# Second attention, projecting steps: transposes and values of every third unit joined with the next unit's small products

## The chip, the cores and the metric

The kernel runs on one core of a Trainium2 chip. The metric is device time in microseconds (us) for one execution; the kernel before takes 1373.73 us, the median of 3 runs (1373.12 to 1374.71). The engines of a core work side by side, each through its own instructions in order, and wait for one another by semaphores: TensorE (PE, with its weight loads shown apart as PEld), VectorE (DVE), ScalarE (ACT), GpSimd (POOL), and SyncE (SP), which issues the loads from memory.

## The reference, cut to what matters

Two transformer blocks run one after the other over 512 tokens of width 1024, all in fp32. The change lies in the second block's attention: 8 "fox" heads of width 64 with a forget gate, and 4 "diff" heads, whose weights are the difference of two softmaxes.

```python
h = _modulate(x, ln1_g[l], sh1, sc1)
u = h @ w_in[l]
fq, fk, fv, fg, dq, dk, dv = jnp.split(u, splits, axis=-1)
fq = _rms(heads(fq, FOX_HEADS, HEAD_DIM_2), fox_qk_g[l, 0])      # fk alike
fox_out = _fox_attention(fq, fk, fv, log_f)    # softmax(q k / 8 + decay, causal) @ v
dq = _rms(dq, diff_qk_g[l, 0])                                    # dk alike
diff_out = _diff_attention(dq[:, :, 0], dq[:, :, 1], dk[:, :, 0], dk[:, :, 1], dv, lam, slopes)
            # (softmax(q1 k1 + alibi) - lam * softmax(q2 k2 + alibi)) @ v, causal
mixed = jnp.concatenate([fox_out..., diff_out...], axis=-1)
x = x + g1[:, None, :] * (mixed @ w_out[l])
```

## The kernel before

Large products are made of three: each operand is split into a rounded high part and a low rest (`w_hi`, `w_lo`, `h_hi`, `h_lo`), and hi x hi, hi x lo and lo x hi are added up in PSUM. ACT makes the high parts of a weight chunk (`to_hi`, L680), DVE the low ones (`to_lo`, L1217).

The second attention goes in steps t = 1 to 4 (the loop `for t in range(1, 5)`, which each engine writes out for itself). Step t attends with the heads of set a = t - 1 (two fox heads and one diff head with its two softmaxes) and, while t < 4, projects queries, keys and values of set t. These three are the **projecting steps**. A step has 12 **units** u = 0 to 11; n = 12a + u counts them through. `UNITS2` gives each unit its kind and its block of 128 queries qb = u // 3: u % 3 = 0 is the diff head (kind 2), u % 3 = 1 and 2 are the two fox heads (kinds 0 and 1). A unit of block qb sees (qb + 1) x 128 keys, so units grow in the course of a step.

A unit passes through this pipeline:

- `scores2(n)` on PE (L2121, in the trace `acc<-qk,qk`) writes q k into the banks `acc2` and `acc3`; for the two fox heads both are made at kind 0, none at kind 1;
- `logits2(n)` on DVE (L1797, `s<-acc,...`) adds the bias, finds the maximum and writes the tile `s_2[n % 3]`;
- ACT makes the exponentials in place (L1030, `s<-s,stat`) and their sum;
- `weights2(n)` on DVE divides (and for kind 2 takes the difference), and signals `p2_ready`;
- `turn2(n)` on PE (L2565, `turn<-consts,s`) transposes qb + 1 blocks into the PSUM bank `turn0`. There is one such bank, so `turn2(n)` waits for `pt2_done`, that is until ACT has copied out the transposes of unit n - 1;
- `turn2_copy(n)` on ACT (L980, `pt<-turn`) copies them to `pt_2[n % 3]` and signals `pt2_done`;
- `values2(n)` on PE (`turn<-pt,v` for the diff head, into the bank `turn1`; `ada<-pt,v` for the fox heads, both at kind 1, none at kind 0) multiplies with the values.

On PE the slot of unit u in a projecting step holds `scores2(n)`, `turn2(n - 2)`, `values2(n - 3)`, and then one twelfth of the projection: 12 products of 512 columns, or 24 of 256 from u = 8 on (the values). At the end of the slots u = 2, 4, 6, 8 `head_squares` follows: two products into the bank `norm` over the squares of a projected query or key.

On ACT, unit u holds, in this order: `turn2_copy(n - 2)`; at u = 0 the squares of the last step's diff head (`diff_square`); at u = 8 the `to_hi` of the chunk after the values; the exponentials of unit n; at u = 2 `fox_round(a - 1)` (L984, the high part of the fox heads' output) and at u = 3 `diff_round(a - 1)`; at u = 1 a `to_hi`; at u = 1, 3, 5, 7 the two `square` operations (L696, L697) of what was just projected, which wait for it; at u = 0 and u = 2, 4, 6, 8 `rstd_start`, three operations (L686, L688, L692) that wait for the norm products; at u = 4 a `to_hi`.

On DVE, unit u holds `logits2(n)`, at u = 4, 6, 8 the rest of the squares (L1272, `sq_lo`), `weights2(n - 1)`, at u = 2 the rest of the squares and a `to_lo`, at u = 3, 5, 7, 9 the scaling of a query or key (which frees its projection bank), at u = 3 `fox_rest(a - 1)` (L1779, `m_lo`), at u = 4 `diff_rest(a - 1)`.

Step 4 doesn't project; it makes half of the first output chunk in place of that, in an order of its own.

Of the kernel before, what the change touches and what calls it, by code (L numbers as in the profile page):

```python
# [154 lines left out]
def program(nc, d):  # L155
# [242 lines left out]
    def norm2(t, mi):  # L398

        return N_2 + 4 * t + max(0, t - 1) + mi  # L400
# [68 lines left out]
    with block:  # L469
# [202 lines left out]
        def _(act):  # L672
# [152 lines left out]
            for c in range(1, NKV // 2):  # L825
                u = W_KV // 2 + c
# [186 lines left out]
            for t in range(1, 5):  # L1013
                w0 = W_Q2 + 3 * t
                a = t - 1
                project = t < 4
                for u in range(12):
                    n = 12 * a + u
                    if n >= 2:
                        turn2_copy(n - 2)  # L1020
                    if a >= 1 and u == 0:
                        diff_square(a - 1)
                    if project and u == 8:
                        to_hi(*divmod(w0 + 3, 2))
                    kind, qb = UNITS2[u]
                    width = (qb + 1) * P
                    sets = 2 if kind == 2 else 1
                    act.wait_ge(s2_freed, 16 * a + s_reads(u)[0] + sets)
                    for e in range(sets):
                        ex = nc.scalar.activation(s_2[n % 3][:, e, 0:width], s_2[n % 3][:, e, 0:width], ACT.Exp, scale=-1.0,  # L1030
                                                  bias=stat2[:, 0, n % 2, e:e + 1], accum_out=stat2[:, 1, n % 2, e:e + 1])
                    ex.then_inc(exp2_done, 1)
                    if a >= 1 and u == 2:
                        fox_round(a - 1)
                    if a >= 1 and u == (3 if project else 7):
                        diff_round(a - 1)
                    if t == 4 and u == 5:
                        to_hi(*divmod(W_OUT2 + 1, 2))
                    if project and u == 1:
                        to_hi(*divmod(w0 + 1, 2))  # L1040
                    if project and u in (1, 3, 5, 7):
                        k = norm2(t, u // 2)
                        act.wait_ge(mm_done, 2 * w0 + u // 2 + 1)
                        act.wait_ge(sum_done, k)
                        square(G[u // 2 % 2], sq_hi_2, sq[0])
                    if a >= 1 and u == (0 if project else 1):
                        rstd_start(norm_d(a - 1), NB[:, :], P)
                    if project and u in (2, 4, 6, 8):
                        rstd_start(norm2(t, u // 2 - 1), NB[:, :], 64)
                    if project and u == 4:  # L1050
                        to_hi(*divmod(w0 + 2, 2))
# [152 lines left out]
        def _(dve):  # L1204
# [579 lines left out]
            def diff_last(a):  # L1784
                newton(norm_d(a), P)
                scale_last(norm_d(a), d_out[:, :])
# [89 lines left out]
            for t in range(1, 5):  # L1876
                w0 = W_Q2 + 3 * t
                a = t - 1
                project = t < 4
                for u in range(13):  # L1880
                    n = 12 * a + u
                    if not project and u == 1:
                        rest2(norm_d(a - 1))
                    if u < 12:
                        logits2(n)
                        if project and u in (4, 6, 8):
                            rest2(norm2(t, u // 2 - 1))
                        if n >= 1:
                            weights2(n - 1)
                    if project and a >= 1 and u == 0:  # L1890
                        rest2(norm_d(a - 1))
                    if project and u == 2:
                        rest2(norm2(t, 0))
                    if project and u == 10:
                        dve.wait_ge(s2_freed, 16 * a + s_reads(10)[0])
                        nc.vector.tensor_scalar(consts[:, K_DIST:K_DIST + TOK], consts[:, K_DIST:K_DIST + TOK], SLOPES_D[t] / SLOPES_D[a], None,
                                                ALU.mult).then_inc(dist_scaled, 1)
                        mask_rows(t)
                    if project and u in (2, 12):
                        to_lo(*divmod(w0 + (1 if u == 2 else 3), 2))  # L1900
                    if a >= 1 and u == (1 if project else 2):
                        diff_first(a - 1)
                    if a >= 1 and u == (1 if project else 5):
                        diff_last(a - 1)
                    if a >= 1 and u == (4 if project else 8):
                        diff_rest(a - 1)
                    if project and u in (3, 5, 7, 9):
                        mi = u // 2 - 1
                        kn, tile = norm2(t, mi), qk[t % 2][mi][:, :]
                        scale_first(kn, tile, G[mi % 2][:, :], gains[:, 1 + mi:2 + mi]).then_inc(acc_freed, 1)  # L1910
                        newton(kn, 64)
                        scale_last(kn, tile)
                    if project and u == 6:
                        to_lo(*divmod(w0 + 2, 2))
                    if a >= 1 and u == 3:
                        fox_rest(a - 1)
                    if project and u in (10, 12):
                        v2_copy(t, u // 2 - 5)
# [200 lines left out]
        def _(pe):  # L2119
# [440 lines left out]
            def turn2(n):  # L2560

                pe.wait_ge(p2_ready, n + 1)
                ge(pe, pt2_done, n)
                for b in range(UNITS2[n % 12][1] + 1):
                    turned = nc.tensor.transpose(T0[:, P * b:P * b + P], s_2[n % 3][:, 0, P * b:P * b + P], ident)  # L2565
                turned.then_inc(turn2_done, 1)
# [51 lines left out]
            for t in range(1, 5):  # L2618
                w0 = W_Q2 + 3 * t
                a = t - 1  # L2620
                project = t < 4
                for u in range(12):
                    n = 12 * a + u
                    if u == 0:

                        pe.wait_ge(acc_freed, 2 * w0 - 18)
                        pe.wait_ge(rstd_done, norm2(a, 3) + 1)
                    if project or u < 2:
                        scores2(n)
                    if n >= 2:  # L2630
                        turn2(n - 2)
                    if not project and u in (2, 5, 6, 8, 9):
                        scores2(n + 1)
                    if n >= 3:
                        values2(n - 3)
                    if not project and u == 3:
                        scores2(n + 1)
                    if project:
                        mi, w = u // 2, w0 + u // 4
                        par = w % 2  # L2640
                        if u % 4 == 0:
                            pe.wait_ge(lo_done, w - 1)
                        if u == 10 or (u % 2 == 0 and mi < 5):
                            pe.wait_ge(acc_freed, 2 * w0 + mi - 17)
                        for part in range(2):
                            if mi < 4:
                                kt0 = 4 * (u % 2) + 2 * part
                                last = columns(G[mi % 2][:, :], par, mi % 2, KT, h_hi, h_lo_of, (kt0, kt0 + 1))
                            else:
                                last = rows(G[mi % 2][:, 256 * (u % 2):256 * (u % 2) + 256], par, u - 8, 0, 256, range(4 * part, 4 * part + 4))  # L2650
                        if u % 2 == 1:
                            last.then_inc(mm_done, 1)
                        if u in (2, 4, 6, 8):
                            head_squares(norm2(t, u // 2 - 1), half_r)
                    if t == 4:

                        half = u % 2
                        if u < 2:
                            pe.wait_ge(lo_done, W_OUT2 - 1)
                            pe.wait_ge(acc_freed, 2 * W_OUT2 + half - 17)  # L2660
                        pe.wait_ge(mlo_done, (4, 4, 4, 4, 5, 6)[u // 2])
                        columns(G[half][:, :], W_OUT2 % 2, half, KT, m_hi, m_lo_of, ((0, 4, 1, 5, 2, 6)[u // 2],))
                    if a >= 1 and u == (0 if project else 1):
                        head_squares(norm_d(a - 1), ones_r)
# [224 lines left out]
```

## Time and profile before

| | |
|---|---|
| median of 3 runs | 1373.73 us (1373.12 to 1374.71) |
| the profiled execution, its own time | 1375.31 us |
| its span, first to last instruction | 1373.5 us |
| PE busy | 1364.8 us, 99% |
| PE weight loads busy | 1169.5 us, 85% |
| DVE busy | 1058.7 us, 77% |
| ACT busy | 718.5 us, 52% |
| POOL busy | 51.0 us, 4% |
| projecting steps 1, 2, 3 | about 812.7 to 965.8 us of the span |

How to read it: the span is from the first to the last instruction of the profiled execution; its own time has a little more around it. Busy time is the sum of an engine's instructions; those of PE overlap, since a product is counted until its last result is out, so PE is shown busy even where the distance between two products is longer than it need be. That distance is read from the starts in the timeline. The chain of work that ended last says which engine sets the end. In a timeline a row gives start, duration, engine, line, operation, tiles (out<-in), shapes and count; equal instructions that follow one another are merged, with their number behind x. In square brackets is the time for which the engine stood idle before, and what ended it.

### The profile page before, as it was taken

To read this page: it belongs to the slowest core of one execution; us is meant where nothing else is said; L and a number is where in the kernel's file an instruction comes from. 1 tells how busy PE (TensorE), PEld (TensorE's weight loads), DVE (VectorE), ACT (ScalarE), POOL (GpSimd) and SP (SyncE) were. 2 spreads that over 40 slices of the span, in tenths; PEclk is the share of its full clock that TensorE was granted. 3 is DMA by queue.
4 is the path that set the end of the run, shared out by engine and by line. 5 is a ranking of instruction groups with operands and counts; after the bars stand their busy time and mean duration, and the time that the engine had idled before them with its cause. 6 is when DMAs were issued, how large, how long until landed. Compare 5 with 4: busy or idle time off the path is not lost.

```text
span 1373.5 us, 21419 instructions
## 1 busy us (share of the span) xinstructions
PE 1364.8 (99%) x7923; PEld 1169.5 (85%) x7923; DVE 1058.7 (77%) x1787; ACT 718.5 (52%) x1260; POOL 51.0 (4%) x55
## 2 busy tenths in 40 slices
PE   8999999999999999999999999999999999999999
PEld 6998888888889878888888787787688998998997
DVE  6976777777899788888888877778867965983883
ACT  4744333223357566666663566766646642662561
POOL 0000000000100000000001100000030000000000
PEclk9999999999999999999999999999999999999999
DMA  9994445457743211112212231111131232333232
GB/s 378 382 354 188 177 181 183 183 201 279 293 155 108 93 62 63 62 62 74 78 62 66 88 124 63 64 60 62 48 107 64 91 123 67 119 123 124 69 116 92
DMA packets 35350, 181.51 MB, mean 132 GB/s; under 512 B 4153, under 2 KB 4921, under 8 KB 20930
## 3 DMA queue, kind: packets, MB, share of 16 engines
q1 hardware_dynamic: 34050, 177.95, 35.7%
q10 hardware_dynamic: 1216, 2.44, 0.6%
q8 instruction: 52, 0.85, 0.3%
q14 instruction: 32, 0.26, 0.1%
HBM read 177.74 MB, written 2.11 MB: 131 GB/s over the span
## 4 chain that ended last, share of the span: by engine, by line
PE 97%; DVE 1%; ACT 1%; issue 0%; DMA 0%; DVEq 0%; ACTq 0%
PE acc L2121 72%; PE turn L2708 7%; PE ada L2121 4%; PE turn L2121 3%; PE norm L2121 3%; PE ada L2708 2%; PE acc L2708 2%; PE norm L2708 2%; PE turn L2565 1%; PE turn L2422 1%; DVE y_half L1209 0%; DVE w_lo L1217 0%; DVE wv_lo L1217 0%; ACT sq L697 0%; DVE k_t L1209 0%
## 5 line engine op out<-in xcount | busy, mean ns | idle before, releaser
L2121 PE MATMUL acc<-h_hi,w_hi 128*128 128x512 f32 x696 | 277.8, 399 | 0.0
L2121 PE MATMUL acc<-h_hi,w_lo 128*128 128x512 f32 x696 | 272.0, 391 | 0.0
L2121 PE MATMUL acc<-h_lo,w_hi 128*128 128x512 f32 x696 | 271.3, 390 | 0.0
L1217 DVE TENSOR_TENSOR w_lo<-w_raw,w_hi 128x2048 fp32r<-128x2048 f32 x58 | 136.4, 2352 | 27.7 <-ACT w_hi L680 27.7
L2121 PEld LDWEIGHTS acc<-h_hi,w_lo 128*128 128x128 f32 x696 | 130.6, 188 | 28.4
L2121 PEld LDWEIGHTS acc<-h_hi,w_hi 128*128 128x128 f32 x696 | 131.0, 188 | 27.1 <-issue 1.2
L2121 PEld LDWEIGHTS acc<-h_lo,w_hi 128*128 128x128 f32 x696 | 130.9, 188 | 25.6
L680 ACT ACTIVATE w_hi<-w_raw 128x2048 fp32r<-128x2048 f32 x60 | 114.3, 1906 | 29.4 <-PE acc L2121 28.6
L1209 DVE SCALAR_TENSOR_TENSOR x<-acc,mods,x 128x512 f32<-128x512 f32 x48 | 38.7, 813 | 68.6 <-PE acc L2121 68.6
L2121 PE MATMUL acc<-wv_hi,h_hi 128*128 128x256 f32 x320 | 90.5, 284 | 0.0
L2121 PE MATMUL acc<-wv_lo,h_hi 128*128 128x256 f32 x320 | 89.1, 279 | 0.0
L2121 PE MATMUL acc<-wv_hi,h_lo 128*128 128x256 f32 x320 | 88.3, 279 | 0.0
L686 ACT ACTIVATE y<-norm,eps_tile 128x512 f32<-128x512 f32 x54 | 37.2, 688 | 72.8 <-PE norm L2121 72.8
L2121 PE MATMUL acc<-gu_lo,w_hi 128*128 128x512 f32 x176 | 68.5, 389 | 0.0
L2121 PE MATMUL acc<-gu_hi,w_hi 128*128 128x512 f32 x176 | 68.5, 389 | 0.0
L2121 PE MATMUL acc<-gu_hi,w_lo 128*128 128x512 f32 x176 | 68.5, 389 | 0.0
L2121 PEld LDWEIGHTS acc<-wv_hi,h_hi 128*128 128x128 f32 x320 | 60.1, 188 | 1.2 <-issue 1.0
L2121 PEld LDWEIGHTS acc<-wv_lo,h_hi 128*128 128x128 f32 x320 | 60.9, 190 | 0.2
L2121 PEld LDWEIGHTS acc<-wv_hi,h_lo 128*128 128x128 f32 x320 | 59.6, 188 | 0.0
L1209 DVE SCALAR_TENSOR_TENSOR ada_out<-ada_out,csil 128x1024 f32<-128x1024 f32 x32 | 38.4, 1221 | 17.2 <-DMA ada_out<-in_ada 16.9
L2121 PE MATMUL acc<-y_hi,w_hi 128*128 128x512 f32 x128 | 49.9, 390 | 0.0
L2121 PE MATMUL acc<-y_hi,w_lo 128*128 128x512 f32 x128 | 49.8, 389 | 0.0
(372 smaller groups left out, 3489.8 us busy)
## 6 DMA issues: line engine op xcount, KB each, us to landing
w_raw<-in_weights SPq DMA_DIRECT2D x102, 1024.0 KB, 4.9
ada_v<-in_ada SPq DMA_DIRECT2D x32, 512.0 KB, 6.3
ada_raw<-in_ada SPq DMA_DIRECT2D x32, 512.0 KB, 5.6
ada_out<-in_ada SPq DMA_DIRECT2D x32, 512.0 KB, 6.5
ada_up<-in_ada_first SPq DMA_DIRECT2D x8, 1024.0 KB, 16.3
w_raw<-in_weights SPq DMA_DIRECT2D x4, 768.0 KB, 4.3
x<-in_x SPq DMA_DIRECT2D x2, 1024.0 KB, 6.1
w_first<-in_weights SPq DMA_DIRECT2D x4, 512.0 KB, 13.3
```

Of the source, the lines that this page charges most:

```text
L680: nc.scalar.activation(weights_at(u, par)[0][:, 0:used], w_raw[par][:, 0:used], ACT.Copy).then_inc(hi_done, 1)
L686: nc.scalar.activation(y0[:, :], total, ACT.Ln, scale=1.0 / count, bias=eps_col).then_inc(ln_done, 1)
L1209: return nc.vector.scalar_tensor_tensor(out, in0, scalar, in1, op0, op1, **more)
L1217: nc.vector.tensor_tensor(lo[:, 0:used], w_raw[par][:, 0:used], f32(hi[:, 0:used]), ALU.subtract).then_inc(lo_done, 1)
L2121: return nc.tensor.matmul(out, lhsT, rhs, start=start, stop=stop)
L2422: turned = nc.tensor.transpose((T0, T1)[c % 2][:, P * b:P * b + P], s_b[tile][:, lo:lo + P], ident)
L2565: turned = nc.tensor.transpose(T0[:, P * b:P * b + P], s_2[n % 3][:, 0, P * b:P * b + P], ident)
L2708: last = nc.tensor.matmul(out, w_part[:, n, :], a_part[:, n, :], start=start and n + m == 0, stop=stop and n + m == 5, skip_group_check=no ...
```

## The change

In the projecting steps PE no longer does `turn2` and `values2` in the slots u % 3 = 2. What stood there goes to the head of the next slot: for n = 3, 6, ..., 36, `turn2(n - 3)` and `values2(n - 4)` come ahead of `scores2(n)`, and `turn2(n - 2)` and `values2(n - 3)` follow it as before. So small products stand in 8 of the 12 slots of a step. The unit n = 36 is the first of step 4.

ACT's copy of the transposes that moved goes with them: `turn2_copy(n - 3)` is now the first thing in the units u % 3 = 0, directly ahead of `turn2_copy(n - 2)`, and the units u % 3 = 2 have none. Since the fox heads' last values of a step come one slot later, `fox_round` goes on ACT from u = 2 to u = 3 and `fox_rest` on DVE from u = 3 to u = 4, ahead of `diff_rest`.

```diff
--- before.py
+++ after.py
@@ -1016,7 +1016,9 @@
                 project = t < 4
                 for u in range(12):
                     n = 12 * a + u
-                    if n >= 2:
+                    if 0 < n <= 36 and u % 3 == 0:
+                        turn2_copy(n - 3)
+                    if n >= 2 and not (project and u % 3 == 2):
                         turn2_copy(n - 2)
                     if a >= 1 and u == 0:
                         diff_square(a - 1)
@@ -1030,7 +1032,7 @@
                         ex = nc.scalar.activation(s_2[n % 3][:, e, 0:width], s_2[n % 3][:, e, 0:width], ACT.Exp, scale=-1.0,
                                                   bias=stat2[:, 0, n % 2, e:e + 1], accum_out=stat2[:, 1, n % 2, e:e + 1])
                     ex.then_inc(exp2_done, 1)
-                    if a >= 1 and u == 2:
+                    if a >= 1 and u == (3 if project else 2):
                         fox_round(a - 1)
                     if a >= 1 and u == (3 if project else 7):
                         diff_round(a - 1)
@@ -1902,6 +1904,8 @@
                         diff_first(a - 1)
                     if a >= 1 and u == (1 if project else 5):
                         diff_last(a - 1)
+                    if a >= 1 and project and u == 4:
+                        fox_rest(a - 1)
                     if a >= 1 and u == (4 if project else 8):
                         diff_rest(a - 1)
                     if project and u in (3, 5, 7, 9):
@@ -1912,7 +1916,7 @@
                         scale_last(kn, tile)
                     if project and u == 6:
                         to_lo(*divmod(w0 + 2, 2))
-                    if a >= 1 and u == 3:
+                    if a >= 1 and not project and u == 3:
                         fox_rest(a - 1)
                     if project and u in (10, 12):
                         v2_copy(t, u // 2 - 5)
@@ -2625,13 +2629,18 @@
 
                         pe.wait_ge(acc_freed, 2 * w0 - 18)
                         pe.wait_ge(rstd_done, norm2(a, 3) + 1)
+                    joined = n <= 36 and u % 3 == 0
+                    if joined and n > 0:
+                        turn2(n - 3)
+                        if n > 3:
+                            values2(n - 4)
                     if project or u < 2:
                         scores2(n)
-                    if n >= 2:
+                    if n >= 2 and not (project and u % 3 == 2):
                         turn2(n - 2)
                     if not project and u in (2, 5, 6, 8, 9):
                         scores2(n + 1)
-                    if n >= 3:
+                    if n >= 3 and not (project and u % 3 == 2):
                         values2(n - 3)
                     if not project and u == 3:
                         scores2(n + 1)
```

## Rows read from the trace of the kernel before

**Rows 1.** The page, chain of work that ended last: shares by engine.
```profile
PE 97%; DVE 1%; ACT 1%; issue 0%; DMA 0%; DVEq 0%; ACTq 0%
```

**Rows 2.** Timeline of PE, step 2, slots 0 to 2: start us, us, engine, line, operation.
```profile
865.75 0.40 PE L2121 MATMUL norm<-sq_lo,ones_r 128*128 128x512 f32 x1
...
866.07 0.49 PE L2121 MATMUL acc<-qk,qk 64*128 64x128 f32 x4
...
869.76 0.27 PE L2565 MATMUL turn<-consts,s 128*128 128x128 f32 x1
869.97 1.09 PE L2121 MATMUL ada<-pt,v 128*64 128x128 f32 x16
870.99 0.50 PE L2121 MATMUL acc<-h_hi,w_hi 128*128 128x512 f32 x1
...
871.33 0.40 PE L2121 MATMUL acc<-h_lo,w_hi 128*128 128x512 f32 x1
```

**Rows 3.** Timeline, step 2, slots 2 and 3: all engines.
```profile
871.87 0.69 DVE L1272 TENSOR_TENSOR sq_lo<-sq,sq_hi 128x512 fp32r<-128x512 f32 x1 [1.52 <-ACT sq L697]
...
873.84 0.39 PE L2121 MATMUL norm<-sq_hi,half_r 128*128 128x512 f32 x1
...
874.51 0.69 ACT L686 ACTIVATE y<-norm,eps_tile 128x512 f32<-128x512 f32 x1 [1.63 <-PE norm L2121]
...
875.03 0.33 PE L2565 MATMUL turn<-consts,s 128*128 128x128 f32 x1
...
876.43 0.26 ACT L980 ACTIVATE pt<-turn 128x128 f32<-128x128 f32 x1
```

**Rows 4.** Timeline, after the steps: PE released by DVE.
```profile
993.33 0.70 DVE L1272 TENSOR_TENSOR sq_lo<-sq,sq_hi 128x512 fp32r<-128x512 f32 x1 [0.41 <-ACT sq L697]
...
994.08 0.50 PE L2121 MATMUL norm<-sq_hi,ones_r 128*128 128x512 f32 x1
```

**Rows 5.** Timeline of PE, step 1, slots 2 and 3.
```profile
822.26 0.39 PE L2121 MATMUL norm<-sq_hi,half_r 128*128 128x512 f32 x1
...
823.45 0.33 PE L2565 MATMUL turn<-consts,s 128*128 128x128 f32 x1
```

**Rows 6.** Timeline of ACT and PE, step 2, slots 5 and 6.
```profile
886.19 0.36 ACT L980 ACTIVATE pt<-turn 128x256 f32<-128x256 f32 x1
...
886.45 0.50 ACT L1030 ACTIVATE s<-s,stat 128x256 f32<-128x256 f32 x1
...
886.75 0.44 PE L2565 MATMUL turn<-consts,s 128*128 128x128 f32 x2
...
887.90 0.39 ACT L980 ACTIVATE pt<-turn 128x256 f32<-128x256 f32 x1
```

**Rows 7.** Timeline of ACT and PE, step 2, slots 8 and 9.
```profile
894.70 0.49 PE L2565 MATMUL turn<-consts,s 128*128 128x128 f32 x3
...
895.87 0.50 ACT L980 ACTIVATE pt<-turn 128x384 f32<-128x384 f32 x1
...
896.24 1.93 ACT L680 ACTIVATE w_hi<-w_raw 128x2048 fp32r<-128x2048 f32 x1
...
898.05 0.62 ACT L1030 ACTIVATE s<-s,stat 128x384 f32<-128x384 f32 x1
...
898.55 0.21 ACT L1030 ACTIVATION_READ_ACCUMULATOR s<-s,stat 128x1 f32 x1
...
900.17 0.55 PE L2565 MATMUL turn<-consts,s 128*128 128x128 f32 x3
```

**Rows 8.** Timeline of ACT and PE, step 2 slot 11, step 3 slot 0.
```profile
908.25 0.60 PE L2565 MATMUL turn<-consts,s 128*128 128x128 f32 x4
...
908.88 0.60 ACT L980 ACTIVATE pt<-turn 128x512 f32<-128x512 f32 x1 [1.74 <-PE turn L2565]
...
910.90 0.72 ACT L1030 ACTIVATE s<-s,stat 128x512 f32<-128x512 f32 x1 [1.42 <-DVE stat L1797]
...
912.94 0.66 PE L2565 MATMUL turn<-consts,s 128*128 128x128 f32 x4
```

## The prediction

> **What bounds the kernel now.** First the chain of the page: almost all of it lies on TensorE (PE) [rows 1]. So time is saved only where PE is spared work, and lost wherever PE is made to wait. Then the timeline of PE in the second attention's projecting steps (t = 1, 2, 3; about 51.6 us each: the same norm product, that of slot 2, stands at 822.26 in step 1 and at 873.84 in step 2 [rows 3, 5]). There each of the 12 units of a step is a slot: a group of small products (scores, transposes, values), then 2.74 us of projecting products (from 870.99 to the norm product at 873.84, less the 0.11 explained below), and after some slots two norm products. I write S, T, V for scores, transposes and values, with the unit's number in the step; P for the projecting part; N(u) for the norm products at the end of slot u. The reader is to see that PE runs through from one slot to the next, and what leaving and entering a group costs [rows 2]. Last, the timeline of ScalarE (ACT) in the same stretch, since T is a single PSUM bank: `turn2` waits until ACT has copied the transposes before it (`pt2_done`), and ACT works in its program's order. Where ACT stands when PE wants the bank is the whole question.
>
> **What the change removes.** In each slot with u % 3 = 2, T and V go out and come back at the head of the next slot. The number of S, T, V and P instructions is unchanged. What goes is one passage P to small and one back. From the last norm product to S it is 866.07 - 865.75 = 0.32 us, and within a run of 512-column products one takes (873.84 - 871.33) / 11 = 0.228 [rows 2, 3], so entering S costs 0.09. Leaving costs at least the slower first product, 870.99 to 871.33 = 0.34, that is 0.11 more. V to P and the new V to S, which the trace of before doesn't show, I take as equal, for both leave a form of another shape. Saving: 0.09 + 0.11 = 0.20 us a join. Its bounds are 0 (V to S, with both shapes changed, costs 0.20 more than V to P) and 0.35: 16 V take 1.09, so one follows another by (1.09 - 0.27) / 15 = 0.055 if the last is as long as a T, 0.27; the last begins at 870.79 and P 0.20 later, 0.15 more than a V would, and that too would go if V to S costs nothing. Joins are at n = 3, 6, ..., 36: 12 of them, so 2.4 us, from 0 to 4.2.
>
> A page bears on this. What the rows show is a first S, whose operands have 64 rows, coming 0.32 after a product of 128 rows rather than 0.23. The Trainium skill, TensorEngine Tiling (Array Packing), section Tiling Modes, Key Properties, says that "Changing tiling mode (not just tile) drains the TensorE". Before, slots 2 and 3 change mode four times around T, V, S and T, after it three times. By that rule alone the change is a gain of the size just worked out, and it would be the rival below.
>
> **What the change adds: a wait in the middle of the joined group.** In slot u = 0, 3, 6, 9 PE now does T(n-3), V(n-4), S(n), T(n-2), V(n-3), P. T(n-2) needs ACT's copy of T(n-3). Before, that copy had a whole slot. Now only V(n-4) and S(n) lie between, and in ACT's order the copy has moved from ahead of exp(n-1) to behind everything that ACT does in slot n-1. Queued behind the waiting T on PE are V, P and all later slots, so each wait goes fully into the time. The four places:
>
> u = 3, steps 2 and 3. ACT ends slot 2 with `rstd_start`, three operations that begin with the norm N(2). P(2) now begins where T(0) stood, 869.76 instead of 870.99, and sheds the 0.11: N(2) would come at 873.84 - 1.34 = 872.50. But it needs `sq_lo`, done at 871.87 + 0.69 = 872.56, whose chain on ACT begins before the moved work; with 0.05 from a DVE end to a PE start [rows 4] N(2) is at 872.61. The first operation follows N by 874.51 - 873.84 = 0.67, the copy follows that by 876.43 - 874.51 = 1.92 and takes 0.26 [rows 3]: it ends at 875.46, so T(1) is at 875.51 where it was at 875.03. Lost 0.48, and twice (step 3 repeats step 2): 0.96.
>
> u = 3, step 1. There is no V(-1), and slot 2 held one transpose only, so N moves just by about 0.1, to 822.16. Copy: 822.16 + 0.67 + 1.92 + 0.26 = 825.01, T(1) at 825.06 where it was at 823.45 [rows 5]. Lost 1.61.
>
> u = 6, all three steps. Before, ACT copied T(3) at 886.19, then exp(5), the two squares of the key, and copied T(4) at 887.90 [rows 6]. Now the first copy is gone from its place (0.26 earlier for what follows: 886.45 - 886.19) and stands behind the squares, at 887.90 - 0.26 = 887.64. It takes 0.36, so T(4) is at 888.05 where it was at 886.75. Lost 1.30 each: 3.90. Cover is missing by much, because ACT comes late from rounding a weight chunk at u = 4.
>
> u = 9, all three steps. exp(8) begins 896.24 - 895.87 = 0.37 earlier, at 897.68, and its read of the sum, 0.50 later, takes 0.21: ACT is free at 898.39. N(8) comes with P(8) from 894.70 on at 897.44, its first follower could be at 898.11, so ACT decides: 898.39 + 1.92 + 0.50 for the copy + 0.05 = 900.86, where T(7) was at 900.17 [rows 3, 7]. Lost 0.69 each: 2.07. DVE's `sq_lo` for N(8) and the bank freed for P(8) may be tight as well, as `sq_lo` was at N(2), which can only add; I price that in rival (b).
>
> u = 0 of the next step, three times. Slot 11 has no work of ACT behind exp(11). T(9) would be at 908.25 + 2.74 = 910.99, its copy could start 908.88 - 908.25 = 0.63 later, at 911.62; ACT is at exp(11) from 910.90 for 0.72 and the read, some 0.1 more, so it copies from about 911.75 to 912.35. T(10) is wanted at 912.94 - 0.20 = 912.74 [rows 8]: no wait, the 0.20 is kept. Gain 0.60.
>
> Sum: 0.96 + 1.61 + 3.90 + 2.07 - 0.60 = 7.94 us, say 7.9. The savings at the nine other joins are not added, since T(n-2) is set by ACT there and no longer by PE. The 0.05 per wait is from DVE to PE (994.08 - 993.33 - 0.70 [rows 4]); for ACT to PE the trace shows no wait so clean, and allow 0 to 0.15, that is -0.5 to +0.9 over nine waits.
>
> The rest moves at nothing. `fox_round` and `fox_rest` go one unit later: each is an operation of 512 columns, about 0.69 by the nearest rows [rows 3], on ACT and DVE, and ACT waits for PE once in each of these slots (the 1.63 in [rows 3] is one such wait); m_lo of a fox head is next read a whole step later, and the V that overwrites its bank moved by a slot too. If that cover were gone, 0.7 per step would be late. No DMA is moved; the weight loads wait on DVE's `lo_done` and PE's pace, both of which only get later. Nothing after unit 36 changes in order, so the delay is carried to the end: the later stages have PE as their bound too, and I see no place that gives it back.
>
> **Rivals.** (a) The passages decide, and the copies are hidden: 12 x 0.20 = 2.4 us faster, 1371.3, and up to 4.2, 1369.5, by the other bound. For it: it is so at u = 0, where ACT's slot ends early. Against it: [rows 3, 6, 7], where ACT's own chain is longer than V + S. It decides if the copy of T(n-3) ends before S(n) does, so at u = 6 by 886.5 instead of 888.0. (b) The waits come, but PE also waits where ACT or DVE now have no slack (N(2), N(8), the freed bank at P(8)), and ACT's lateness is carried from one join into the next: twice more per step at up to 0.3, and 0.15 for each released T, about 2.7 us on top: 1384.4. For it: the 0.06 by which `sq_lo` already misses N(2). Against it: each of ACT's stretches begins again with something that PE releases (1.63 of waiting in [rows 3]), so lateness isn't carried. (c) The two sides nearly cancel: the copies are in time at u = 6 (3.90 less, and 0.60 saved) and at u = 3 of step 1 (1.61 less), which leaves 1.8: 1375.6. It would need ACT to be some 1.3 us earlier against PE at both places than its rows have it.
>
> **How the numbers follow.** The profiled execution took 1375.31 us (span 1373.5); plus 7.9 it would be 1383.3, span 1381.4. It stands 1.6 above the median of the runs, 1373.73, and the difference carries over: 1381.7. Chances: my forecast 0.74, (b) 0.15, (a) 0.06, (c) 0.05. The range leaves out (a) and (c) and the tails: below, 1378.7, if u = 6 costs 0.7 instead of 1.3 and u = 3 of the first step 0.9 instead of 1.6 (-2.5) with the smaller gap per wait (-0.5); above, 1385.0, (b) with a little more. A measurement of this kernel can tell about 0.2% (2.75 us) from no change. Slower by more than that: 0.89, from the forecast and (b); within: 0.07, (c) and the part of (a) with 0.20 a join, whose 2.4 us just miss the bound; faster: 0.04, (a) with more than 0.23 a join.
>
> **What would show it.** In the profile after: TensorE's list of waits gets "turn <- ACT pt" with nine entries of about 0.5 to 1.6 us, and the group `turn<-consts,s` the idle time; the T behind S at u = 6 is 1.3 later against its S than before, at u = 9 0.7, at u = 0 it is not. The number of matmuls stays. A step from `turn` to `turn` grows from 51.6 to about 53.9. From V straight to S shows the price of that passage: 0.20 from the last V if my 0.20 a join is right. The forecast is wrong if the copies lie before the squares, if PE has no idle at these places, or if the steps grow by less than 1.

## The result, and the profile after

The changed kernel takes 1381.44 us (median of 6 runs, 1381.32 to 1382.36), the kernel before 1373.14 beside it: 8.3 us slower, a ratio of 1.006 with a 95% interval of 1.0049 to 1.0071. The forecast was 1381.7.

The page of the kernel after, engines and shares of the chain, and then TensorE's list of waits (us in total, times, longest):

```profile
PE 1361.7 (99%) x7923; PEld 1166.6 (85%) x7923; DVE 1058.9 (77%) x1787; ACT 718.5 (52%) x1260; POOL 50.9 (4%) x55
PE 87%; DMA 3%; ACT 3%; DVE 3%; issue 2%; SPq 0%; DVEq 0%; ACTq 0%
```
```profile
PE turn L2569 <- ACT pt L980: 9.2, 9, 1.6
```

The work is the same, PE is still shown 99% busy, but nine waits of T for ACT's copy are new, at the nine places that the sum named. ACT's share of the chain rose from 1% to 3% [rows 1], since the chain goes through ACT wherever T waits. Most of PE's fall from 97% to 87% is something else, which differs from trace to trace: in the run join_u0 below, in which no T waits for a copy in these steps, the chain has these shares:

```profile
PE 90%; DMA 3%; DVE 3%; issue 1%; ACT 1%; SPq 0%; DVEq 0%; ACTq 0%
```

The first and the last S of the second attention tell where the time went. First before, then after; the columns are the durations of one, least/median/most, in ns, and the first and last start in us:

```profile
L2121 PE MATMUL acc<-qk,qk x128: 272/482/693, 812.7 to 985.3; 64*128 64x128 f32 x32, 64*128 64x256 f32 x32, 64*128 64x384 f32 x32, 64*128 64x512 f32 x32
```
```profile
L2125 PE MATMUL acc<-qk,qk x128: 272/482/693, 810.3 to 991.5; 64*128 64x128 f32 x32, 64*128 64x256 f32 x32, 64*128 64x384 f32 x32, 64*128 64x512 f32 x32
```

I call this stretch the stage: 172.6 us before, 181.2 after, 8.6 longer. That is the whole loss of 8.3, to within 0.3. That the stage of before begins 2.4 later is no effect of the change: its profiled execution (1375.31) lost those 2.4 us ahead of the stage, and stands 2.2 above the median of all runs shown beside it, 1373.14. The profiled execution of after, 1381.5, stands at its median. So the step from span to span, 6.2, understates the change, and from here on the stage is compared with the stage.

The timelines of step 2 after, at u = 3, 6, 9 and at u = 0 of step 3, beside [rows 3, 6, 7, 8]:

```profile
873.35 0.39 PE L2125 MATMUL acc<-h_hi,w_lo 128*128 128x512 f32 x1
873.72 0.50 PE L2125 MATMUL norm<-sq_hi,half_r 128*128 128x512 f32 x1
874.06 0.40 PE L2125 MATMUL norm<-sq_lo,half_r 128*128 128x512 f32 x1
874.49 1.09 PE L2125 MATMUL ada<-pt,v 128*64 128x128 f32 x16
874.49 0.69 ACT L686 ACTIVATE y<-norm,eps_tile 128x512 f32<-128x512 f32 x1 [1.17 <-PE norm L2125]
875.51 0.70 PE L2125 MATMUL acc<-qk,qk 64*128 64x256 f32 x4
876.41 0.26 ACT L980 ACTIVATE pt<-turn 128x128 f32<-128x128 f32 x1
876.81 0.30 PE L2569 MATMUL turn<-consts,s 128*128 128x128 f32 x1 [0.59 <-ACT pt L980]
...
887.51 0.92 PE L2125 MATMUL acc<-qk,qk 64*128 64x384 f32 x4
888.95 0.58 ACT L697 ACTIVATE sq<-acc 128x512 f32<-128x512 f32 x1
889.43 0.38 ACT L980 ACTIVATE pt<-turn 128x256 f32<-128x256 f32 x1
889.96 0.41 PE L2569 MATMUL turn<-consts,s 128*128 128x128 f32 x2 [1.53 <-ACT pt L980]
...
901.43 0.68 ACT L686 ACTIVATE y<-norm,eps_tile 128x512 f32<-128x512 f32 x1
903.34 0.47 ACT L980 ACTIVATE pt<-turn 128x384 f32<-128x384 f32 x1
903.96 0.52 PE L2569 MATMUL turn<-consts,s 128*128 128x128 f32 x3 [0.61 <-ACT pt L980]
...
915.46 0.58 ACT L980 ACTIVATE pt<-turn 128x512 f32<-128x512 f32 x1
916.14 0.49 PE L2125 MATMUL acc<-qk,qk 64*128 64x128 f32 x4
916.56 0.66 PE L2569 MATMUL turn<-consts,s 128*128 128x128 f32 x4
```

Read the bracket on T: it can start only when the copy above it is done. At u = 0 there is no bracket; the copy, 915.46 + 0.58, was done before T was wanted. The same T stood at 875.03, 886.75, 900.17 and 912.94 before, so it lies 1.78, 3.21, 3.79 and 3.62 later; from one to the next +1.43, +0.58, -0.17, and +0.65 for the first against the T(10) ahead of it (862.49 after, 861.36 before). Over all three steps, with the forecast in parentheses: u = 3 of step 1 +1.64 (1.61), u = 3 of steps 2 and 3 +0.65 and +0.63 (0.48 each), u = 6 +1.44, 1.43, 1.45 (1.30), u = 9 +0.71, 0.58, 0.64 (0.69), u = 0 -0.25, -0.17, -0.16 (-0.20). Sum 8.6 against 7.94. From one step to the next, the T of u = 3 stands at 876.81 and 930.87, 54.1 apart, where 53.9 were forecast and 51.6 is the value of before.

### The profile page after: what moved, and what is told of

Its sections match the earlier page's. It is cut to its first block, busy times and chain, and to the rows that moved or that the text cites. A ratio compares the mean times of both kernels' runs of the same rounds, so it can differ in the third digit from the quotient of the medians.

```text
span 1379.7 us, 21419 instructions
## 1 busy us (share of the span) xinstructions
PE 1361.7 (99%) x7923; PEld 1166.6 (85%) x7923; DVE 1058.9 (77%) x1787; ACT 718.5 (52%) x1260; POOL 50.9 (4%) x55
## 4 chain that ended last, share of the span: by engine, by line
PE 87%; DMA 3%; ACT 3%; DVE 3%; issue 2%; SPq 0%; DVEq 0%; ACTq 0%
PE acc L2125 64%; PE turn L2717 7%; PE ada L2125 4%; DMA ada_out<-in_ada 3%; PE turn L2125 3%; PE norm L2125 2%; PE ada L2717 2%; PE acc L2717 2%; PE norm L2717 2%; DVE w_lo L1219 1%; PE turn L2569 1%; PE turn L2426 1%; ACT y L686 1%; ACT wv_hi L680 1%; ACT y L688 1%
```

## The experiments

Two theories. **The waits**: TensorE waits straight for ACT's copy, nine times, and each such wait goes in full into the time; without them the change gains what the passages save. **Against it**: my rival (b), that late norms, freed banks and lateness handed on carry a good part; and rival (a), that only passages count. All runs are compared with runs of the kernel before on the same chip. The stage below is from the first to the last S of each run's own trace.

### copies_both: the copies ahead again, the groups still joined

```diff
-                    if 0 < n <= 36 and u % 3 == 0:
+                    if 0 < n <= 36 and u == 0:
                         turn2_copy(n - 3)
-                    if n >= 2 and not (project and u % 3 == 2):
+                    if n >= 2 and not (project and u in (2, 8, 11)):
                         turn2_copy(n - 2)
...
+                    if project and u in (2, 8):
+                        turn2_copy(n - 2)
                     if project and u in (2, 4, 6, 8):
                         rstd_start(norm2(t, u // 2 - 1), NB[:, :], 64)
```

> The changed kernel, its joined groups on TensorE untouched; only ScalarE's order differs: the copy of T(3) stands ahead of exp(5) again, and those of T(0) and T(6) ahead of rstd_start of slots 2 and 8. If the nine waits of TensorE for the copies are the whole loss (8.6 us of the stage), they go, and the passages saved stay, 0.20 each at 12 joins: 1381.4 - 8.6 - 2.4 = 1370.5 us, 2.5 faster than before, and no row of TensorE waiting for pt longer than 0.2. If the loss comes from norms or freed banks that are late (my rival b), at least 2 us of it stay: 1372.5 or more. If passages save nothing, 1373.1.

Measured: 1373.14 us against 1373.20, ratio 1.000 (0.9991 to 1.0009); stage 172.0. The loss is gone with nothing but the order of ACT changed, so the waits were the loss. But the stage is only 0.6 shorter than before and not 2.4. The trace of this run tells why. At the end of slot 2, at u = 6 and at the start of P(8), step 2:

```profile
868.76 0.39 PE L2127 MATMUL acc<-h_hi,w_lo 128*128 128x512 f32 x1
869.13 0.50 PE L2127 MATMUL norm<-sq_hi,half_r 128*128 128x512 f32 x1
869.47 0.39 PE L2127 MATMUL norm<-sq_lo,half_r 128*128 128x512 f32 x1
...
882.22 0.92 PE L2127 MATMUL acc<-qk,qk 64*128 64x384 f32 x4
882.70 0.36 ACT L980 ACTIVATE pt<-turn 128x256 f32<-128x256 f32 x1
883.21 0.41 PE L2571 MATMUL turn<-consts,s 128*128 128x128 f32 x2
...
890.27 0.74 DVE L1213 SCALAR_TENSOR_TENSOR qk<-acc,gains,y 128x512 f32<-128x512 f32 x1
890.88 0.39 PE L2127 MATMUL acc<-h_hi,w_lo 128*128 128x512 f32 x1
891.16 0.36 PE L2127 MATMUL acc<-wv_hi,h_hi 128*128 128x256 f32 x1
```

N(2) comes 0.37 after the last P in place of 0.23, and its second product 0.34 after the first: 0.14 of waiting for the squares, and then 0.11 for a slow first product, as after any break. S to T takes 0.99 in place of 0.84. P(8) begins 0.28 after the last product ahead of it, so 0.05 late, and 0.15 after DVE has freed its bank (890.27 + 0.74), and has 0.08 of a slow first product too. N(8) of step 1 waits for the squares as well, 0.14 in all. And the products of slots 10 and 11 take 5.74 us together, 901.76 to 907.50, where they take 5.55 in the trace of after. That is 2 x 0.25 + 3 x (0.15 + 0.13) + 0.14 + 3 x 0.19 = 2.05 us, of which 0.57 is slower spacing of products, with no wait and no cause found: the saving of 2.4 is eaten almost whole.

### copies_squares and copies_rstd: one kind of place at a time

copies_squares puts only the copy of T(3) back (`u in (0, 3, 9)` and `u in (2, 8, 11)` in the two conditions), copies_rstd only those of T(0) and T(6).

> Of the three places only u = 6 is put right: ScalarE copies T(3) ahead of exp(5), so not behind the two squares. ScalarE is rounding a weight chunk until 886.2 on the axis of the trace before, the copy ends at 886.55, T(4) is wanted at 886.55 and comes at 886.7, 0.05 ahead of its old place, in place of 1.44 behind it: three times 1.5 less, 1377.0 us. The waits at u = 3 and u = 9 stay as long as they are (1.6, 0.65, 0.63 and about 0.65 behind their old places). If waits share a cause and pass from one to the next, those at u = 9 shrink too and it is under 1376.

Measured: 1377.46 us, 4.3 above before (ratio 1.0028, 1.0018 to 1.0038), stage 176.8; T waits 6 times. The gain of 4.4 in the stage is the one expected, and the waits at u = 9 stay.

> Only u = 3 and u = 9 are put right: the copies of T(0) and T(6) stand ahead of the three operations of rstd_start. They were 1.64 + 0.65 + 0.63 and 0.71 + 0.58 + 0.64 = 4.85 behind their old places and come 0.20 ahead of them: 4.85 + 1.2 = 6.0 less, 1375.4 us, the waits at u = 6 unchanged at 1.4 to 1.6. The norm's chain starts up to 0.5 later behind its sums; if that is on the path (the bank of the key, the query of the next step), it is 1376 or more.

Measured: 1377.24 us, 4.0 above before (1.0027, 1.0018 to 1.0036), stage 176.4, 4.8 us less than after where 6.0 were expected. T waits 3 times, S to T at u = 6 is 2.45 as in after. What is missing are again the savings, 0.20 at each join, not the waits. The lists of the two runs, copies_squares first, then copies_rstd:

```profile
PE turn L2569 <- ACT pt L980: 4.6, 6, 1.6
```
```profile
PE turn L2571 <- ACT pt L980: 4.6, 3, 1.5
```

The two add up to the nine waits of after, 4.6 + 4.6 = 9.2: each place stands for itself, and nothing is handed from one to the next. The stage says the same: 4.4 and 4.8 us less than after, and with both orders changed 181.2 - 172.0 = 9.2. That part of rival (b) is out.

### round_later: why ACT is late at u = 6

```diff
+                    if project and u == 6:
+                        to_hi(*divmod(w0 + 2, 2))
...
-                    if project and u == 4:
-                        to_hi(*divmod(w0 + 2, 2))
```

> ScalarE's rounding of the weight chunk moves from u = 4 to u = 6, behind the two copies there; the order of exp(5), squares, copy of T(3) is the changed kernel's. My claim is that ScalarE is late at u = 6 because of this rounding, 1.9 us. Then the squares begin when P(5) is done, the copy ends at about 886.55 on the old axis, T(4) comes at 886.7 in place of 888.2: 4.3 less, 1377.1 us. If the order alone is at fault (copy behind the squares), the wait stays over 1 us and the time within 1 us of 1381.4. If the chunk is now late for P(8), a new wait of TensorE for wv_lo appears at u = 8.

Measured: 1377.62 us (ratio 1.0034, 1.0021 to 1.0047), stage 177.0. The copy still lies behind the squares, yet the waits at u = 6 are gone from the list (6 left, 4.6 us); S to T there is 1.03, where 0.84 is the value of before, so 0.2 is left of each. So the order makes the wait possible and the rounding of the chunk, 1.9 us just before, makes it long. No wait for `wv_lo` appeared.

### extra_op: one more operation ahead of each moved copy

```diff
-            def turn2_copy(n):
...
+            def turn2_copy(n, extra=False):
...
                 act.wait_ge(turn2_done, n + 1)
                 width = (UNITS2[n % 12][1] + 1) * P
+                if extra:
...
+                    nc.scalar.activation(spare[:, :], T0[:, :], ACT.Copy).then_inc(spare_done, 1)
...
-                        turn2_copy(n - 3)
+                        turn2_copy(n - 3, True)
```

> The changed kernel with one more operation of ScalarE, a copy of 512 columns to an unused tile, about 0.48 from its start to the next, ahead of each moved copy (at all 12 joins). If TensorE waits straight for the copy at u = 3, 6, 9, each of these nine waits grows by the whole 0.48, 4.3 us; at u = 0, where the copy had 0.2 to spare by my sum, by 0.25 to 0.3, another 0.8: 1386.5 us in all, 5.1 slower than the changed kernel. If the waits were only partly the copy's, it grows by less than 3 us.

Measured: 1390.98 us (ratio 1.0123, 1.0106 to 1.014), stage 189.0: 9.5 slower than the changed kernel by the medians and 7.8 by the stage, where 5.1 were expected. TensorE's list, and then four of its waits, those of 2.0 or longer, in the timeline:

```profile
PE turn L2577 <- ACT pt L988: 13.6, 9, 2.1
```
```profile
825.94 0.30 PE L2577 MATMUL turn<-consts,s 128*128 128x128 f32 x1 [2.10 <-ACT pt L988]
841.23 0.41 PE L2577 MATMUL turn<-consts,s 128*128 128x128 f32 x2 [2.02 <-ACT pt L988]
896.87 0.41 PE L2577 MATMUL turn<-consts,s 128*128 128x128 f32 x2 [2.02 <-ACT pt L988]
952.53 0.41 PE L2577 MATMUL turn<-consts,s 128*128 128x128 f32 x2 [2.02 <-ACT pt L988]
```

The waits grew by 13.6 - 9.2 = 4.4 us, as expected for a straight wait, and at u = 0 S to T went from 0.42 to 0.53: 0.11 each, 0.3 in all, so the copy there had more to spare than the 0.2 of my sum. The other 3.1 us of the stage are something that no theory had. The windows before, in and after the first wait, behind the second and third of these four, and behind the last, and two products in the third window. A row has the window and its length, the busy us of PE, PEld, DVE, ACT and POOL, the granted clock, the DMA share and GB/s:

```profile
818.00:822.90 4.90, 4.90 (x23) 4.01 (x22) 2.55 (x7) 3.10 (x5) 0.00 (x0) 1.00 0.00 0
823.00:825.90 2.90, 0.84 (x6) 0.30 (x4) 2.86 (x9) 2.60 (x5) 0.00 (x0) 1.00 0.31 45
827.00:830.40 3.40, 3.40 (x9) 2.65 (x9) 0.04 (x1) 0.53 (x3) 0.00 (x0) 0.50 0.32 133
841.40:845.00 3.60, 3.60 (x20) 2.97 (x18) 2.31 (x2) 1.57 (x5) 0.00 (x0) 1.00 0.23 32
897.00:900.50 3.50, 3.50 (x19) 3.00 (x19) 2.35 (x2) 1.58 (x5) 0.00 (x0) 1.00 0.16 21
953.20:956.50 3.30, 3.30 (x10) 2.59 (x9) 1.81 (x1) 1.35 (x5) 0.00 (x0) 0.51 0.24 40
```
```profile
827.52 0.63 PE L2133 MATMUL acc<-h_lo,w_hi 128*128 128x512 f32 x1
827.95 0.63 PE L2133 MATMUL acc<-h_hi,w_lo 128*128 128x512 f32 x1
```

After the first wait, 2.10 us long, and after the last, 2.02, TensorE's granted clock was 0.50 (1.2 GHz), and the products came 0.43 apart in place of 0.23; each time it cost 1.6 us. The two other waits of 2.02, with the same work around them, left the clock at 1.00. In the trace of after, with waits up to 1.61, the clock is 1.00 all along. The four runs of this kernel differ in it: their mean granted clocks are 0.998 (the profiled one), 0.996, 0.997 and 0.999, where every run of every other kernel here has 1.0. So the number of such stretches changes from run to run, and which of these waits brings one is open. That may also be why the medians give 9.5 and the stage of the one trace 7.8, but no run here shows it.

### join_u0: joins only where no wait came

The kernel before with the join at n = 12, 24 and 36 alone, on PE and ACT.

> The kernel before with joins only at u = 0 (n = 12, 24, 36), where no wait for the copy came. Passage theory: 0.20 a join, the stage 0.6 us shorter by its trace, within noise by its time: 1372.6. In copies_both the 48 products of the values that now follow one another in slots 10 and 11 took 5.74 us in place of 5.57. If that comes from running without a break, it shows here too and eats nearly all: the stage no more than 0.1 shorter. If not, spacing in slots 10 and 11 stays 0.114 and the whole 0.6 is there.

Measured: 1372.57 us against 1373.55 (ratio 0.9992, 0.9983 to 1.0001, not told apart from no change), stage 171.9, 0.7 shorter. Taken from the first S to the S of unit 36, which stops ahead of step 4, it is 0.72: 0.24 for each join. V, S and T of this run at the join of step 2:

```profile
860.07 0.88 PE L2123 MATMUL ada<-pt,v 128*64 128x128 f32 x12
860.87 0.49 PE L2123 MATMUL acc<-qk,qk 64*128 64x128 f32 x4
861.29 0.66 PE L2567 MATMUL turn<-consts,s 128*128 128x128 f32 x4
```

The passages do save what was said. And the products in slots 10 and 11 kept their spacing of 0.114, so running without a break is not what slowed them in copies_both.

### fox_late: the part priced at nothing

`fox_round` and `fox_rest` one unit later in the kernel before, nothing else.

> The kernel before with fox_round and fox_rest one unit later and nothing else, the part that I priced at nothing. Cover theory: the stage from its first scores to those of step 4 stays at 151.4 us within 0.1, the time within 0.1% of before. Without cover it would be 0.7 in steps 2 and 3, 1.4 us slower.

Measured: 1373.25 us against 1373.55 (1.0001, 0.9991 to 1.001), stage 172.6, that of before. It costs nothing.

### rounds_moved: the two chunks behind the squares

```diff
-                    if project and u == 1:
-                        to_hi(*divmod(w0 + 1, 2))
                     if project and u in (1, 3, 5, 7):
...
                         square(G[u // 2 % 2], sq_hi_2, sq[0])
+                    if project and u == 1:
+                        to_hi(*divmod(w0 + 1, 2))
+                    if project and u == 5:
+                        to_hi(*divmod(w0 + 2, 2))
...
-                    if project and u == 4:
-                        to_hi(*divmod(w0 + 2, 2))
```

> copies_both, with the two weight chunks of slots 1 and 4 rounded behind the squares of units 1 and 5 in place of ahead of them. In copies_both TensorE lost 0.14 + 0.11 at N(2) of steps 2 and 3 (squares late, then a slow first product) and 0.14 at T(4) of each step, 0.9 us, both through ScalarE rounding a chunk just before. If so, these go: the stage 151.4 - 0.57 - 0.9 = 149.9 us, 1.5 shorter than before, the time about 1371.7, 0.1% faster than before and at the edge of what can be told. If the losses only move to the exponentials of units 2 and 6, the stage stays at 150.8 or more.

Measured: 1371.92 us against 1373.55, ratio 0.9987 (0.9978 to 0.9995), 1.6 us or 0.13% faster than before, and the stage 171.1, 1.5 shorter, as expected. N(2), and S and T at u = 6, of step 2 in this run:

```profile
871.58 0.39 PE L2127 MATMUL acc<-h_hi,w_lo 128*128 128x512 f32 x1
871.81 0.39 PE L2127 MATMUL norm<-sq_hi,half_r 128*128 128x512 f32 x1
...
884.79 0.92 PE L2127 MATMUL acc<-qk,qk 64*128 64x384 f32 x4
885.64 0.44 PE L2571 MATMUL turn<-consts,s 128*128 128x128 f32 x2
```

N(2) follows the last P by 0.23 and T follows S by 0.85, as before the change: neither waits any more. This is the version that beats both kernels, by little. The spacing of the products changed too, but both ways, and nearly cancels: slots 10 and 11 of step 1 have the shorter one again, and slot 8 has the longer one in all steps.

## Why the prediction was right, point by point

**The nine waits.** Right in place, cause and number. Undoing ACT's order alone (copies_both) took the whole loss back, each kind of place answered by itself, and lengthening ACT by one operation lengthened all nine waits by it, 0.49 each.

**Their sizes.** 8.6 in the stage against 7.94. The term that was too small is the gap from the end of ACT's copy to T. I took 0.05, from DVE to PE [rows 4]. It is 0.15: 889.43 + 0.38 = 889.81, T at 889.96; so too at 876.41 + 0.26 and 903.34 + 0.47. Nine times 0.10 is 0.9, the upper end of what I had allowed. The rest, -0.2, is small things of both signs. At u = 9 I had ACT begin the three operations when its read of the sum had ended; in step 2 that is at 901.53, and they begin at 901.43, and the copy takes 0.47 and not 0.50. At u = 3 of steps 2 and 3 it is the 0.11 below. So the sum is right in part because errors of both signs met, and the time of 1381.44 lies still nearer to 1381.7 because the median from which I started, 1373.73, was 0.6 above that of all six runs, 1373.14.

**u = 6, "because ACT comes late from rounding a weight chunk".** Shown by round_later.

**u = 0.** No wait and 0.16 to 0.25 saved, against 0.20; the slack that I gave the copy was too small, without consequence.

**N(2).** I had it wait for `sq_lo` until 872.61 on the old axis, 0.11 after it was wanted, and it did wait, 0.14. What the step missed is that a product after a wait is slow like one after a passage (873.72 to 874.06, 0.34), another 0.11.

**0.20 a passage.** Right as a price: V to S, which the trace of before didn't show, is 0.20 from the last V (16 V in 1.09 from 874.49, the last at 875.31, S at 875.51), just as V to P, and join_u0 gave 0.24 a join. The Trainium skill, TensorEngine Tiling (Array Packing), section Tiling Modes, says that a change of mode drains TensorE. The runs agree so far as they show that a change costs time, and put about 0.2 us on a passage out and back with fp32 operands. As a forecast for rival (a) it would have been wrong: even without the waits the 12 joins gave 0.6 and not 2.4 (copies_both), since PE, a little ahead, runs into the next engine that had been hidden, which is 1.5 us by the list at copies_both, and since slots 10 and 11 ran at a slower spacing, 0.57 us, which isn't explained.

**What moves at nothing.** Shown for `fox_round` and `fox_rest` (fox_late).

**Rival (b)** had a true core, N(2) and P(8), worth 0.25 and 0.13 where they occur, but its handing on of lateness is out, and in the changed kernel these are within the sum. **Rival (c)** didn't come about.

## What to carry to other kernels

Joining small products to save passages puts their round trips through another engine into one group: ask for each which operation of the other engine now stands between, and read from the timeline when that engine is free, not how busy it is (ACT: 52%). Where an operation is moved on the engine that sets the time, its partner on the others must be moved with regard to what stands around it there; here the place of nine copies in ACT's order was worth 9.2 us of the stage (after against copies_both). And a small saving on the bound engine, 0.2 us twelve times, is kept at most as far as the next engine has slack: here a quarter of it, and a good half once two roundings were out of the way.

## What the runs showed of the hardware that I had not expected

- After waits of 2.10 and 2.02 us TensorE fell to a granted clock of 0.50 (827.0 to 830.4, 953.2 to 956.5), at 1.6 us each; after two others of 2.02 it did not, and never after waits up to 1.61 (extra_op, after). By the mean clocks, how many do it changes from run to run. A wait that grows from 1.6 to 2.1 can thus cost four times what it adds. The Trainium skill, TensorE: Matmul & The Clock Gate, section Back-to-back issue gap, gives a product of N columns N/1.2 ns at the low clock, 0.427 us for 512; the rows show 0.43.
- From the end of ACT's copy to the T that waits for it is 0.14 to 0.15 us, nine times in the trace of after. From DVE's end to PE it is 0.05 where a norm product waits for `sq_lo` [rows 4], but 0.15 where P(8) waits for its bank (copies_both: 891.01 to 891.16). So it isn't a matter of the engine, and one of these can't be taken for the other; what decides is open.
- The first product after a wait takes 0.08 to 0.11 longer until the next, like the first after a change of shape.
- The products of 256 columns run at one of two spacings within a slot, 0.114 or 0.118 us, at the same granted clock. In the trace of before all slots have the first, in copies_both slots 10 and 11 of all steps the second; in the trace of after it is slot 9 of steps 2 and 3 and slot 8 of step 3. What chooses is open; join_u0 excludes that it is the lack of a break.
